# Four experts in two passes, and one of the six weight blocks of a three-pass step multiplied in native fp32 without a split

## The chip, the cores and the metric

The kernel runs on one core of a Trainium2 chip. The metric is the time of one execution on the device, in microseconds, the median of a few runs. One profiled execution gives the trace that is read below.

## What is computed

A two-layer encoder on 256 tokens of width 1024 in fp32: an attention layer and a dense SwiGLU layer, a second attention layer, and a top-2-of-8 mixture of experts. The change lies wholly in the last:

```python
logits = (xt @ w_router).astype(jnp.float32)
top_val, top_idx = lax.top_k(logits, TOP_K)
top_w = jax.nn.softmax(top_val, axis=-1)
...
y = jnp.zeros_like(xt)
for e in range(N_EXPERTS):
    y = y + gates[:, e:e + 1] * swiglu(xt, w_gate[e], w_up[e], w_down[e])
```

Each expert has a gate and an up matrix of 1024 x 3584 and a down matrix of 3584 x 1024. With 8 experts that is 8 x 3 x 3584 x 1024 x 4 bytes = 352.3 MB of weights, each read once.

## The kernel before

**Units.** The weights come in units of 128 x 2048 fp32 (1 MiB). A step is one slice of 512 hidden columns of one expert: two gate units, two up units, two down units. An expert has 7 steps, so the stage has 56 steps and 336 units. SyncE loads the units in the order in which they are used into `raw`, a ring of `RING = 6` buffers. The order is: four gate and up units of step n, then the two down units of step n-1, then the next step. Unit i goes into the buffer of unit i-6.

**Split.** To keep fp32 accuracy on the fast fp32r products, each unit is split in two: ScalarE rounds it to `w_hi` (`hi`, line 623), VectorE subtracts to get `w_lo` (`lo`, line 1169) and counts `lo_done`. The two halves go to one of four places (three in `w_hi`/`w_lo`, a fourth in `qk_hi`/`qk_lo`). ScalarE waits until TensorE has used what stood there (`used`). SyncE waits for `lo_done` of unit i-6 before it loads unit i: the ring buffer is free as soon as it has been split, long before TensorE gets to it.

**Passes.** The tokens of an expert are gathered to at most 96 slots. A three-pass ("big") expert multiplies hi x hi, lo x hi and hi x lo (`three`, lines 1887 to 1889): 12 products of 128x512 for a unit. A two-pass ("small") expert has at most 64 tokens; hi and lo parts of its tokens stand side by side in one 128-wide stationary operand, which takes 8 products for a unit, and a product with a shift matrix (`shifted`, line 2462) that adds the lower half to the upper, twice in a step.

**Order of steps.** A rank by token count picks the experts: five big (`BIG_V`) and three small (`SMALL_V`). `SMALL_AFTER` says behind which big step each small step stands. In iteration n TensorE does gate and up of step n, then down of step n-1 (`step_down`), then the transposes of step n's hidden values (`step_turn`, lines 2341 and 2505). The rows of an expert are gathered and its results added to memory by GpSimd's indirect DMAs (lines 2675 and 2685).

The first step's down units are units 8 and 9, the second's 14 and 15; the second down unit of the step at position n has number 6(n+1)+3.

## Time and profile before

| | |
|---|---|
| median of 3 runs | 1368.86 us (1365.44 to 1369.8) |
| span of the profiled execution | 1365.5 us |
| TensorE busy | 1331.8 us, 98% |
| VectorE busy | 1107.3 us, 81% |
| ScalarE busy | 975.5 us, 71% |
| bytes moved by DMA | 433.24 MB |

The shares are means over the whole span. The expert stage takes the last 63% of it, and it is the stage that counts here: its loads begin at 383.8 us with pauses and run without one from about 490 to 1335 us. TensorE's granted clock is 1.00 in this stage. Matmul records overlap, so the distance from start to start is the cost of one, not its duration.

### The profile page before, as it was taken

What the parts mean: (1) busy time and instruction counts of PE and PEld (TensorE: products, weight loads), DVE (VectorE), ACT (ScalarE), POOL (GpSimd) and SP (SyncE); (2) the same over time, 40 slices, a digit from 0 to 9 for tenths busy, and PEclk for the clock granted to TensorE, in tenths of its full rate; (3) what the DMA queues carried; (4) which work ended last, traced back from release to release, by engine and by line L of the source; (5) the groups of instructions that cost most, each with busy time, mean ns of one, the idle gap of its engine ahead of it and who ended that gap; (6) DMA issues with size and microseconds to landing.
All of it is one profiled execution on the core that took longest, in us unless ns stands there. A gap on an engine that the chain in (4) does not pass through costs nothing.

```text
span 1365.5 us, 18288 instructions
## 1 busy us (share of the span) xinstructions
PE 1331.8 (98%) x7233; PEld 1123.6 (82%) x7233; DVE 1107.3 (81%) x885; ACT 975.5 (71%) x930; POOL 168.7 (12%) x103
## 2 busy tenths in 40 slices
PE   8989999999999999999999999999999999999996
PEld 7888999999999778777877888777877877787784
DVE  4664655555666599999999989999999999999995
ACT  5465544446556667888788878888888888878883
POOL 4251000000000132574400000000000000000001
PEclk8999999999999999999999999999999999999998
DMA  9305755554542389999999999999999999999992
GB/s 372 121 1 185 207 186 184 184 184 154 204 144 86 111 332 401 404 419 407 412 421 419 421 401 390 422 421 421 408 411 421 414 411 421 421 411 422 418 418 98
DMA packets 67203, 433.24 MB, mean 317 GB/s; under 512 B 8160, under 2 KB 10336, under 8 KB 18992
## 3 DMA queue, kind: packets, MB, share of 16 engines
q1 hardware_dynamic: 60320, 418.01, 76.4%
q0 software_dynamic: 3360, 12.22, 3.0%
q10 hardware_dynamic: 3440, 1.91, 0.8%
q8 instruction: 51, 0.84, 0.3%
q14 instruction: 32, 0.26, 0.1%
HBM read 426.09 MB, written 6.03 MB: 316 GB/s over the span
## 4 chain that ended last, share of the span: by engine, by line
PE 74%; DVE 11%; DMA 9%; ACT 4%; issue 1%; SPq 0%; DVEq 0%; ACTq 0%
PE banks L1887 21%; PE banks L1889 20%; PE banks L1888 20%; DMA raw<-in_moe_w_gate 9%; DVE w_lo L1169 6%; ACT w_hi L623 2%; PE banks L2451 2%; DVE qk_lo L1169 2%; PE banks L2120 2%; PE banks L2452 2%; ACT qk_hi L623 1%; PE banks L2108 1%; PE banks L2488 1%; PE banks L2490 1%; PE banks L2462 1%
## 5 line engine op out<-in xcount | busy, mean ns | idle before, releaser
L1169 DVE TENSOR_TENSOR w_lo<-raw,w_hi 128x2048 fp32r<-128x2048 f32 (+1 forms) x312 | 711.2, 2297 | 134.4 <-ACT w_hi L623 132.9
L623 ACT CAST w_hi<-raw 128x2048 fp32r<-128x2048 f32 (+1 forms) x312 | 592.5, 1909 | 161.8 <-PE banks L1889 125.5
L1169 DVE TENSOR_TENSOR qk_lo<-raw,qk_hi 128x2048 fp32r<-128x2048 f32 x84 | 192.0, 2286 | 13.0 <-ACT qk_hi L623 12.1
L623 ACT CAST qk_hi<-raw 128x2048 fp32r<-128x2048 f32 x84 | 160.0, 1905 | 14.3 <-PE banks L1889 9.5
L1887 PE MATMUL banks<-w_hi,t_hi 128*128 128x512 f32 (+2 forms) x444 | 164.7, 371 | 2.9 <-DVE w_lo L1169 1.5
L1889 PE MATMUL banks<-w_lo,t_hi 128*128 128x512 f32 (+2 forms) x444 | 161.6, 364 | 0.0
L1888 PE MATMUL banks<-w_hi,t_lo 128*128 128x512 f32 (+2 forms) x444 | 161.5, 364 | 0.0
L1887 PE MATMUL banks<-t_hi,w_hi 128*128 128x256 f32 x544 | 155.5, 286 | 0.9 <-DVE t_lo L1190 0.9
L1888 PE MATMUL banks<-t_hi,w_lo 128*128 128x256 f32 x544 | 154.3, 284 | 0.0
L1889 PE MATMUL banks<-t_lo,w_hi 128*128 128x256 f32 x544 | 154.2, 284 | 0.0
L1887 PE MATMUL banks<-w_hi,h_hi 128*128 128x512 f32 x300 | 118.8, 396 | 0.2 <-DVE w_lo L1169 0.2
L1889 PE MATMUL banks<-w_lo,h_hi 128*128 128x512 f32 x300 | 117.3, 391 | 0.0
L1888 PE MATMUL banks<-w_hi,h_lo 128*128 128x512 f32 x300 | 117.1, 390 | 0.0
L1887 PEld LDWEIGHTS banks<-t_hi,w_hi 128*128 128x128 f32 x544 | 104.7, 192 | 1.9 <-issue 1.4
L1888 PEld LDWEIGHTS banks<-t_hi,w_lo 128*128 128x128 f32 x544 | 104.7, 192 | 0.4
L1889 PEld LDWEIGHTS banks<-t_lo,w_hi 128*128 128x128 f32 x544 | 104.7, 192 | 0.0
L2451 PE MATMUL banks<-w_hi,t_hi 128*128 128x512 f32 x252 | 101.4, 402 | 2.7 <-DVE w_lo L1169 2.5
L1887 PEld LDWEIGHTS banks<-w_hi,t_hi 128*128 128x128 f32 x444 | 85.8, 193 | 16.2 <-DVE w_lo L1169 1.7
L2452 PE MATMUL banks<-w_lo,t_hi 128*128 128x512 f32 x252 | 98.5, 391 | 0.0
L1889 PEld LDWEIGHTS banks<-w_lo,t_hi 128*128 128x128 f32 x444 | 85.9, 193 | 12.9
L1888 PEld LDWEIGHTS banks<-w_hi,t_lo 128*128 128x128 f32 x444 | 86.0, 194 | 12.1 <-issue 0.2
L2685 POOL DMA_INDIRECT moe_sum<-arena x7 | 12.4, 1772 | 497.8 <-ACT arena L1086 497.8
(358 smaller groups left out, 2261.9 us busy)
## 6 DMA issues: line engine op xcount, KB each, us to landing
raw<-in_moe_w_gate SPq DMA_DIRECT2D x112, 1024.0 KB, 9.9
raw<-in_moe_w_up SPq DMA_DIRECT2D x112, 1024.0 KB, 9.3
raw<-in_moe_w_down SPq DMA_DIRECT2D x112, 1024.0 KB, 9.7
raw<-in_na_w_qkv SPq DMA_DIRECT2D x12, 1024.0 KB, 4.8
raw<-in_ffn_w_gate SPq DMA_DIRECT2D x11, 1024.0 KB, 5.0
raw<-in_ffn_w_up SPq DMA_DIRECT2D x11, 1024.0 KB, 5.1
raw<-in_ffn_w_down SPq DMA_DIRECT2D x11, 1024.0 KB, 4.9
raw<-in_w_in_e SPq DMA_DIRECT2D x6, 1024.0 KB, 15.7
```

Source lines behind the costliest of these rows:

```text
L623: act.copy(tile_hi(u, n), raw[:, u.raw, 0:n]).then_inc(hi_done, 1)
L1169: dve.tensor_tensor(tile_lo(u, n), raw[:, u.raw, 0:n], tile_hi(u, n).bitcast(F32), ALU.subtract).then_inc(lo_done, 1)
L1887: pe.matmul(out, a_hi, b_hi, start=start, stop=False)
L1888: pe.matmul(out, a_lo, b_hi, start=False, stop=False)
L1889: return pe.matmul(out, a_hi, b_lo, start=False, stop=stop)
L2108: last = pe.transpose(banks[:, T_BANK[n % 2], (2 * k + t) * P:(2 * k + t + 1) * P], prob_of(n)[:, b, t * SEQ + k * P:t * SEQ + (k + 1) * P ...
L2120: last = pe.matmul(banks[:, 4 + t, c:c + HD], turned_of(n)[:, (2 * k + t) * P:(2 * k + t + 1) * P], v(k), start=(k == 0), stop=(k == 1))
L2451: pe.matmul(dst, t_small[:, kk, :], hi_w[:, k, :], start=kk == 0, stop=False)
L2452: last = pe.matmul(dst, t_small[:, kk, :], lo_w[:, k, :], start=False, stop=kk == KD - 1)
L2462: pe.matmul(banks[:, 4 + i, :], shift, low[i], start=False, stop=True, skip_group_check=True).then_inc(shift_mm, 1)
L2488: pe.matmul(banks[:, 2 + c, :], lhs, hi_w[:, k, cols], start=j == 0 and i == 0 and k == 0, stop=False)
L2490: last = pe.matmul(banks[:, 2 + c, :], lhs, lo_w[:, k, cols], start=False, stop=j == MOE_STEPS - 1 and i == 1 and k == 1)
```

## The change

There are now four big and four small experts (`BIG_V`, `SMALL_V`, `RANK_OF`), and 28 + 28 steps in place of 35 + 21. The order: four big steps first, then big and small steps in turn, with pairs of small steps between, and three big steps at the end. In the middle no two big steps stand next to each other.

`WHOLE` lists the second down unit of each big step but those of the last two: 26 units. Such a unit isn't split. TensorE multiplies it from its ring buffer in native fp32 with `h_whole`, an fp32 copy of that half of the hidden values; ScalarE and VectorE skip it, and only half of the hidden values is split. Its ring buffer becomes free when TensorE has used it (`used`), so the load six units on waits for that. Counts on `lo_done` and `hi_done` leave these units out, and the four places of split units are dealt among the rest. The low halves of small results (`low_y`) move to another buffer.

```diff
-BIG_V, SMALL_V = (0, 2, 3, 5, 7), (1, 4, 6)
-SMALL_AFTER = ((3, 4, 5, 6, 8, 9, 10), (15, 16, 17, 18, 20, 21, 22), (24, 25, 26, 27, 29, 30, 31))
+BIG_V, SMALL_V = (0, 2, 4, 7), (1, 3, 5, 6)
+SMALL_AFTER = ((3, 4, 5, 6, 7, 8, 8), (9, 10, 11, 12, 13, 13, 14), (15, 15, 16, 16, 17, 17, 18),
+               (19, 20, 20, 21, 22, 23, 24))
...
+WHOLE = [6 * (n + 1) + 3 for n, (v, _) in enumerate(ORDER[:-2]) if v in BIG_V]
+SPLIT = [i for i in range(6 * STEPS) if i not in WHOLE]
...
+    def split(self, ahead=0):
+
+        return self.count(ahead) - self.whole
...
+        h_whole = part_of(8448, 2 * P).rearrange("p (k s) -> p k s", k=2)
...
+            def load_moe(i, src):
+
+                u = moe_unit(i)
+                if i - RING in WHOLE:
+                    sp.wait_ge(used, u.count(-RING))
+                elif i >= RING:
+                    sp.wait_ge(lo_done, moe_unit(i - RING).split())
+                else:
+                    sp.wait_ge(lo_done, u.count(-RING))
+                sp.dma_start(raw[:, u.raw, 0:src.shape[-1]], src).then_inc(raw_full[u.raw], 16)
...
+                elif 6 * (n + 1) + 3 in WHOLE:
+                    act.copy(inner(h_hi, 0)[:, 0:2], turned_in()[:, 0:2])
+                    act.copy(h_whole[:, :, 0:SLOTS], turned_in()[:, 2:4]).then_inc(h_hi_done, 1)
...
+            def step_lo(i):
+
+                if i not in WHOLE:
+                    lo(moe_unit(i))
...
+                elif 6 * (n + 1) + 3 in WHOLE:
+                    dve.tensor_tensor(inner(h_lo, 0)[:, 0:2], turned_in()[:, 0:2], inner(h_hi, 0)[:, 0:2].bitcast(F32),
+                                      ALU.subtract).then_inc(h_lo_done, 1)
...
-                    moe_down(U_MOE, [(0, first_unit + i, 0) for i in range(2)], n, start=j == 0,
-                             stop=j == MOE_STEPS - 1, which=which)
+                    if 0 in which:
+                        moe_down(U_MOE, [(0, first_unit, 0)], n, start=j == 0, which=(0,))
+                    if 1 in which:
+                        u = moe_unit(first_unit + 1)
+                        pe.wait_ge(raw_full[u.raw], u.filled())
+                        for k in range(2):
+                            for c in range(2):
+                                last = pe.matmul(banks[:, c, :], h_whole[:, k, :],
+                                                 raw[:, u.raw, k * D + c * HALF:k * D + (c + 1) * HALF], start=False,
+                                                 stop=j == MOE_STEPS - 1 and k == 1)
+                        last.then_inc(used, 1)
```

SyncE's queue where units 10 to 21 are loaded, before (the second of the two `down` loads is unit 15, and further on unit 21):

```order
L526 DMA raw<-in_moe_w_gate 128x2048 [waits lo_done] x2
L526 DMA raw<-in_moe_w_up 128x2048 [waits lo_done] x2
L526 DMA raw<-in_moe_w_down 128x2048 [waits lo_done] x2
L526 DMA raw<-in_moe_w_gate 128x2048 [waits lo_done] x2
L526 DMA raw<-in_moe_w_up 128x2048 [waits lo_done] x2
L526 DMA raw<-in_moe_w_down 128x2048 [waits lo_done] x2
```

The same place after; line 583 is in `load_moe`:

```order
L583 DMA raw<-in_moe_w_gate 128x2048 [waits lo_done] x2
L583 DMA raw<-in_moe_w_up 128x2048 [waits lo_done] x2
L583 DMA raw<-in_moe_w_down 128x2048 [waits lo_done]
L583 DMA raw<-in_moe_w_down 128x2048 [waits used]
L583 DMA raw<-in_moe_w_gate 128x2048 [waits lo_done] x2
L583 DMA raw<-in_moe_w_up 128x2048 [waits lo_done] x2
L583 DMA raw<-in_moe_w_down 128x2048 [waits lo_done]
L583 DMA raw<-in_moe_w_down 128x2048 [waits used]
```

Units 15 and 21 now wait for `used`, which is TensorE's count, and the loads behind them on the queue wait with them.

TensorE at the end of the first small step's iteration (position 4; `banks` is PSUM, `h_hi` and `h_lo` the hidden values, `tab,arena` the identity and the values to be turned), before: the second down unit of the big step ahead of it, then the small step's transposes (line 2505):

```order
L1889 MATMUL banks<-w_lo,h_hi 128x512
L2462 MATMUL banks<-qk_lo,qk_hi 128x512 [waits low_set]
L1887 MATMUL banks<-qk_hi,h_hi 128x512 [waits lo_done,h_lo_done,h_hi_done]
L1888 MATMUL banks<-qk_hi,h_lo 128x512
L1889 MATMUL banks<-qk_lo,h_hi 128x512
...
L1887 MATMUL banks<-qk_hi,h_hi 128x512
L1888 MATMUL banks<-qk_hi,h_lo 128x512
L1889 MATMUL banks<-qk_lo,h_hi 128x512
L2505 MATMUL banks<-tab,arena 128x64 [waits hid_done]
L2505 MATMUL banks<-tab,arena 128x64 x3
```

The same place after; line 2555 is the native product of `raw` with `h_whole` in `arena`, and line 2565 the transposes:

```order
L1938 MATMUL banks<-qk_hi,h_lo 128x512
L1939 MATMUL banks<-qk_lo,h_hi 128x512
L2512 MATMUL banks<-qk_lo,qk_hi 128x512 [waits low_set]
L2555 MATMUL banks<-raw,arena 128x512 [waits raw_full4]
L2555 MATMUL banks<-raw,arena 128x512 x3
L2565 MATMUL banks<-tab,arena 128x64 [waits hid_done]
L2565 MATMUL banks<-tab,arena 128x64 x3
```

The twelve products of the split unit have become four native ones, behind the same second shift product, and their wait is for the load itself and no longer for VectorE.

## Rows read from the trace of the kernel before

**Rows 1.** The page, part 2: bandwidth moved in 40 slices of 34.1 us.
```profile
GB/s 372 121 1 185 207 186 184 184 184 154 204 144 86 111 332 401 404 419 407 412 421 419 421 401 390 422 421 421 408 411 421 414 411 421 421 411 422 418 418 98
```

**Rows 2.** Windows view: start:end, length, busy us by engine, clock, DMA share, GB/s.
```profile
core 0: us, PE busy (x) PEld busy (x) DVE busy (x) ACT busy (x) POOL busy (x), PEclk, DMA share, GB/s
...
1205.00:1325.00 120.00, 118.81 (x525) 94.23 (x524) 115.45 (x64) 103.04 (x75) 0.00 (x0) 1.00 1.01 421
...
1190.00:1200.00 10.00, 10.00 (x46) 8.19 (x45) 9.21 (x6) 7.96 (x5) 1.97 (x1) 1.00 1.02 381
```

**Rows 3.** DMA issues in 480 to 1366 us: count, median us from issue to landing.
```profile
arena<-x_rows,arena POOLq DMA_INDIRECT x7, 9.4
moe_sum<-arena POOLq DMA_INDIRECT x7, 9.3
```

**Rows 4.** Waits of the SyncE queue, 540 to 1350 us: total, times, longest.
```profile
SPq L526 <- DVE w_lo L1169: 470.8, 230, 3.7
```

**Rows 5.** Groups by form, 540 to 1350 us: busy us, mean ns, idle before.
```profile
L1169 DVE TENSOR_TENSOR w_lo<-raw,w_hi 128x2048 fp32r<-128x2048 f32 x234 | 529.9, 2285 | 25.6 <-ACT w_hi L623 24.0
L623 ACT CAST w_hi<-raw 128x2048 fp32r<-128x2048 f32 x234 | 444.9, 1912 | 71.7 <-PE banks L1889 35.8 <-DMA raw<-in_moe_w_down 15.5 <-DMA raw<-in_moe_w_gate 11.3
```

**Rows 6.** Timeline of one steady cycle: start us, us, engine line op [idle before].
```profile
1253.71 1.91 ACT L623 CAST w_hi<-raw 128x2048 fp32r<-128x2048 f32 x1 [0.57 <-DMA raw<-in_moe_w_down]
...
1258.68 1.92 ACT L623 CAST w_hi<-raw 128x2048 fp32r<-128x2048 f32 x1 [0.52 <-DMA raw<-in_moe_w_gate]
...
1260.62 0.58 ACT L1043 CAST qk_lo<-banks 64x512 fp32r<-64x512 f32 x1
...
1261.26 0.50 PE L2462 MATMUL banks<-qk_lo,qk_hi 128*128 128x512 f32 x1 [0.17 <-ACT qk_lo L1043]
...
1261.60 0.39 PE L1887 MATMUL banks<-qk_hi,h_hi 128*128 128x512 f32 x1
...
1264.14 0.40 PE L1889 MATMUL banks<-qk_lo,h_hi 128*128 128x512 f32 x1
```

**Rows 7.** Timeline of TensorE: the transposes that end the first five later steps.
```profile
508.46 0.33 PE L2341 MATMUL banks<-tab,arena 96*128 96x96 f32 x2
...
525.67 0.33 PE L2341 MATMUL banks<-tab,arena 96*128 96x96 f32 x2
...
543.33 0.41 PE L2341 MATMUL banks<-tab,arena 96*128 96x96 f32 x3
...
557.50 0.40 PE L2505 MATMUL banks<-tab,arena 64*128 64x64 f32 x3
...
572.65 0.33 PE L2341 MATMUL banks<-tab,arena 96*128 96x96 f32 x2
```

**Rows 8.** Line L526 in two windows of one load each: issue time, time to landing.
```profile
L526 SPq DMA_DIRECT2D raw<-in_moe_w_down x1: 327/327/327, 502.3 to 502.3; - x1
...
DMA to landing us min/median/max: 6.7/6.7/6.7
...
L526 SPq DMA_DIRECT2D raw<-in_moe_w_down x1: 338/338/338, 536.0 to 536.0; - x1
...
DMA to landing us min/median/max: 8.6/8.6/8.6
```

**Rows 9.** Tile raw in 380 to 500 us: loads that had the queue nearly alone.
```profile
DMA to landing us min/median/max: 4.7/4.9/7.3
```

**Rows 10.** Line L2052, native fp32 128x512: duration, first and last start, records.
```profile
L2052 PE MATMUL banks<-arena x8: 591/592/593, 57.1 to 60.1; 128*128 128x512 f32 x8
```

**Rows 11.** Timeline of TensorE: end of the last steps and last down product.
```profile
1309.38 0.41 PE L2341 MATMUL banks<-tab,arena 96*128 96x96 f32 x3
...
1326.72 0.25 PE L2341 MATMUL banks<-tab,arena 96*128 96x96 f32 x1
...
1349.46 0.40 PE L1889 MATMUL banks<-qk_lo,h_hi 128*128 128x512 f32 x1
```

More of the change, by code:

```diff
@@ L68, in step_order @@
         for v, after in zip(SMALL_V, SMALL_AFTER):
-            if m in after:
-                order.append((v, after.index(m)))
+            for j, at in enumerate(after):
+                if at == m:
+                    order.append((v, j))
     return order
@@ L90, with whole_before @@
     MOVE_AT.setdefault(max(n for n, w in TURN_AT.items() if w[0] == _v - 1), []).append(_v)
+WHOLE = [6 * (n + 1) + 3 for n, (v, _) in enumerate(ORDER[:-2]) if v in BIG_V]
+SPLIT = [i for i in range(6 * STEPS) if i not in WHOLE]
+def whole_before(i):
+    return sum(1 for w in WHOLE if w < i)
 def turned_count(n):
@@ L183, with __init__ @@
 class Unit:
-    def __init__(self, s, k=0, part=None, behind=PARTS):
-        self.s, self.k, self.own, self.behind = s, k, part, behind
+    def __init__(self, s, k=0, part=None, behind=PARTS, whole=0):
+        self.s, self.k, self.own, self.behind, self.whole = s, k, part, behind, whole
     def count(self, ahead=0):
         return self.k * RING + (self.s + 1 + ahead)
+    def split(self, ahead=0):
+        return self.count(ahead) - self.whole
     def early(self, back):
@@ L334, in trunk @@
         low = [qk_lo[:, 3072 + HALF * i:3072 + HALF * (i + 1)] for i in range(2)]
+        low_y = [t_lo[:, 4 * i:4 * i + 4, P:2 * P] for i in range(2)]
         shift = qk_hi[:, 3584:3584 + P]
@@ L498, in moe_unit @@
         def moe_unit(i):
-            turn = i % (PARTS + 1)
-            return Unit(U_MOE + i, 0, (U_MOE + turn) % PARTS if turn < PARTS else PARTS,
-                        PARTS if i < PARTS else PARTS + 1)
+            q = i - whole_before(i)
+            turn = q % (PARTS + 1)
+            behind = PARTS if q < PARTS else PARTS + 1 if q == PARTS else i - SPLIT[q - PARTS - 1]
+            return Unit(U_MOE + i, 0, (U_MOE + turn) % PARTS if turn < PARTS else PARTS, behind, whole_before(i))
         def unit_of(base, e, c, j=0):
@@ L584, in last @@
                 down(e, MOE_STEPS - 1, base, [(e, 40 + i, 0) for i in range(2)])
-            gate_up(0, 0, U_MOE, [(0, i, 0) for i in range(4)])
+            for i, w in enumerate((moe_w_gate, moe_w_gate, moe_w_up, moe_w_up)):
+                load_moe(i, w[0, 0, i % 2])
             expert = {0: 0}
@@ L601, in _ @@
             with sp.If(n_over > SLOTS):
+                sp.wait_ge(used, U_MOE + E * MOE_UNITS)
                 for again in range(1, SWEEPS):
@@ L1123, in _ @@
                     y_low_copy(n)
[L1124 to L1125 removed]
+                step_hi(6 * n + 3)
+                step_hi(6 * n + 4)
                 if j == 0:
@@ L1166, in lo @@
             def lo(u, n=UNIT):
-                dve.wait_ge(hi_done, u.count())
+                dve.wait_ge(hi_done, u.split())
                 dve.tensor_tensor(tile_lo(u, n), raw[:, u.raw, 0:n], tile_hi(u, n).bitcast(F32),
@@ L1917, in columns @@
             def columns(u, bank, n, transposed, split=None):
-                pe.wait_ge(lo_done, u.count())
+                pe.wait_ge(lo_done, u.split())
                 hi_w, lo_w = unit_parts(u, KD, n)
@@ L1936, in rows @@
             def rows(u, bank, lhs_hi, lhs_lo, n_t, start, stop):
-                pe.wait_ge(lo_done, u.count())
+                pe.wait_ge(lo_done, u.split())
                 hi_w, lo_w = unit_parts(u, 2, D)
@@ L1949, in rows_by_half @@
             def rows_by_half(u, bank, lhs_hi, lhs_lo):
-                pe.wait_ge(lo_done, u.count())
+                pe.wait_ge(lo_done, u.split())
                 hi_w, lo_w = unit_parts(u, 2, D)
@@ L2317, in gate_up @@
                     u = unit_of(base, *units[i])
-                    pe.wait_ge(lo_done, u.count())
+                    pe.wait_ge(lo_done, u.split())
                     hi_w, lo_w = unit_parts(u, 4, HALF)
@@ L2442, in step_gate_up @@
                     u = moe_unit(6 * n - 2 + i if n else i)
-                    pe.wait_ge(lo_done, u.count())
+                    pe.wait_ge(lo_done, u.split())
                     hi_w, lo_w = unit_parts(u, 4, HALF)
@@ L2467, in y_shifts @@
                     pe.wait_ge(y_low_set, 2 * SMALL_V.index(v) + i + 1)
-                    pe.matmul(banks[:, 2 + i, :], shift, low[i], start=False, stop=True, skip_group_check=True).then_inc(y_shift_mm, 1)
+                    pe.matmul(banks[:, 2 + i, :].rearrange("p (k s) -> p k s", k=4), shift, low_y[i], start=False,
+                              stop=True, skip_group_check=True).then_inc(y_shift_mm, 1)
             def step_down(n, which=(0, 1)):
@@ L2481, in step_down @@
                         u = moe_unit(first_unit + i)
-                        pe.wait_ge(lo_done, u.count())
+                        pe.wait_ge(lo_done, u.split())
                         hi_w, lo_w = unit_parts(u, 2, D)
```

74 lines of the change are left out of this document (39 added, 35 removed).

## The prediction

> **What bounds the kernel now.** I read the page's bandwidth row first. From slice 18 on it stands between 390 and 422 GB/s to the end of the stage [rows 1]. The windows view says what that means: over 120 quiet microseconds all 16 DMA engines are busy (share 1.01) at 421 GB/s, and the rate drops, to 381, only in a window that holds one of GpSimd's 14 indirect DMAs [rows 2, 3]. In the steady cycle ScalarE starts on one unit and on the second one after it as they land, at 1253.71 and 1258.68 [rows 6], so a unit takes 2.49 us; 1.0486 MB by 421 GB/s is the same 2.49. The stage's 336 units are 837 us of stream. TensorE (118.8 of 120 us busy) and VectorE (115.5) stand almost as high, but in that window both follow the landings. SyncE's long waits for VectorE [rows 4] are no loss: the loads that it issues queue behind others, and the median indirect DMA too takes 9 us to land. So three engines are nearly full and one of them, DMA, is the floor: what the change takes from TensorE and VectorE buys nothing beyond that floor. What it can do is empty the queue.
>
> **What it takes away.** VectorE loses 26 subtractions of 2.29 us and ScalarE 26 copies of 1.91 us [rows 5], 60 and 50 us. ScalarE copies the hidden values in two pieces instead of one, a few tenths more each. TensorE: twelve products run from 1261.60 to 1264.14 [rows 6], eleven distances, 0.23 us each, 2.8 us for a big unit with the last. A small step has 48 of these in place of 72 and two shift products more, so seven steps more in two passes save 7 x 22 x 0.23 = 35 us. The new operation is there in the trace: line 2052 makes four native fp32 products of 128x512, recorded as eight, with starts from 57.1 to 60.1 [rows 10]: 0.43 us a record, 0.86 a product, 3.43 us for the four of a unit. That is 0.7 us more than the split unit, 26 times: 18 us. TensorE ends up some 17 us shorter. All of this lies beside the stream, and I cost it at nothing. Were the stream no cover, it would be TensorE's 17 us that counted.
>
> The Trainium skill (FP8 and Floating Point Precision, TensorE Precision Notes) gives true fp32 four passes. Four times 0.23 would be 3.7 us for a unit rather than 3.43, and the sum below would be 1.1 us higher; the row shows the product itself, so I stay with it.
>
> **What it adds: a wait of the loads.** Unit 6(n+1)+3 (call it w) now keeps its buffer until TensorE has used it. Load w+6 waits for that, and on SyncE's queue all loads behind it. How late may it be? A load that has the queue nearly alone lands after 4.7 to 4.9 us [rows 9], and w+6 is due 6 x 2.49 = 14.9 us after w. So no DMA time is lost while TensorE ends w within about 10.1 us of w's landing. Two places differ.
>
> *In the middle* a small step follows each big one, and the lag is the least possible. In the cycle of rows 6 w landed at 1256.2 (half way between the two landings shown). Before w TensorE does the second shift product, at 1261.26; it waits for ScalarE's copy at 1260.62, behind the copy of unit w+1, which landed at 1258.68. Splitting w is not on that path. Then w starts at 1261.6, and with 3.43 us it ends at 1265.0, 8.8 us after landing. That leaves 1.3 us of slack. TensorE keeps this lag: behind a big step a small one's iteration took 14.2 us (543.33 to 557.50) and a big one's behind a small one 15.2 (to 572.65) [rows 7]; with 0.7 more the pair takes 30.1 by these rows, against 29.8 for twelve landings. These two iterations hold gather transposes and slot products, about 0.6 us in all; without them it is 29.5. A pair of small steps gives 3 us back. I cost the 22 or so of these waits at nothing. Bounds: nothing, or 1.3 us each if the queue runs less well with two or three loads in it than with four, 29 us. I take nothing, since the load of 502.3 had two others in flight and landed after 6.7 us, and a steady queue is seen with that [rows 8].
>
> *At the start* there are four big steps in a row, and TensorE runs behind. Rows 7 give the ends of units 9, 15, 21 and 27: 508.46, 525.67, 543.33 and 557.50. The load that needs unit 9's buffer was issued after the load of 502.3, at 504.5, and that of unit 27 at 536.0, 7.3 us before TensorE was through with unit 21 [rows 8]. With one native unit more each time these ends become 509.2, 527.1, 545.4 and 560.3. Load 27 can be issued at 545.4 and lands 4.8 later, at 550.2; before, it landed at 536.0 + 8.6 = 544.6. So the stream is 5.6 us behind from there, and lost DMA time never comes back. The earlier two waits are part of this and not added (at the first, unit 14 landed at 509.0, so load 15 comes 2.6 us late). The wait for unit 27 (560.3) is in time: unit 32, before w+6, is now due at 564.7. After that TensorE catches up. Bounds of this term: 2 us, if the delayed loads close up where a gather had slowed them (the two gathers at 520 to 555 cost 2 to 3 us in all), and 7, if each wait adds its own.
>
> The Trainium skill (DMA: Bandwidth & Descriptors, Anatomy of one DMA) puts a DMA's fixed part at about 2.0 us besides its bytes, on GpSimd's path. With 2.0 + 2.49 = 4.5 in place of the 4.8 shown here, the start would cost 0.3 us less.
>
> **The end.** The last three steps are big in both orders. Before, TensorE turned at 1309.38 and 1326.72, 17.3 us apart, and its last product is at 1349.46 [rows 11]: it never waits there. The native unit of the step at position 53 falls in this stretch: 0.7 us. The last two big steps are unchanged. **The adds to memory:** one expert sends 64 rows in place of 96. A window with one such DMA moves 381 instead of 421 [rows 2], 1 us lost; a third less is 0.5 us with the tail of it.
>
> **Sum:** 5.6 + 0.7 - 0.5 = 5.8 us over the profiled execution's 1365.5, so 1371.3 of span. That execution stands 3.4 us below the median of the runs, at their lower end; the same 5.8 on the median of 1368.9 gives 1374.7.
>
> **The rivals.**
> - *A queue that runs thin at every wait* (slower). If a load issued 6 us before its due time doesn't keep 16 engines full, each of 22 waits costs 0.5 to 1.3 us: 11 to 29 us more, 1386 to 1403. It decides once TensorE's lag passes 10.1 us, or the latency of a lone load passes 6.1. Against it: 1.3 us of slack; for it: a stage that has always had four loads in flight, and disturbances (gathers, row transposes) of 0.5 us.
> - *The start costs little* (no change). TensorE's first lag falls in time with the two gathers, which slow the stream anyway; then 2 us or less remain: 1369 to 1371.
> - *The floor gives* (faster). The 421 GB/s may not be DMA's own limit but what is left beside 26 fewer reads of `raw` and writes of both halves; or the indirect DMAs cost less. If the stream became shorter by TensorE's 17 us, it would end at 1374.7 - 17 = 1358. Against it: the rate is 418 to 422 in quiet slices whatever the other engines do [rows 1], and no row shows the stream above 422.
> - *It does something else.* The fourth smallest expert must have at most 64 tokens or all is swept again, at hundreds of microseconds. The reference's router gives 53, 58, 62, 62, 64, 64, 73 and 76 tokens, so it fits.
>
> **How the numbers follow.** Forecast 1374.7, chance 0.50, its own range 1371 to 1378. Start costs little 0.25. Thin queue 0.15. Floor gives 0.09. Something else 0.01. Within 0.3% (about what a measurement of this kernel can tell from no change) is 1364.8 to 1373.0: it takes all of the second case and a quarter of the forecast, 0.37. Faster 0.09, slower 0.38 + 0.15 + 0.01, 0.54. The range leaves out the fast case and the worse half of the thin queue: 1368 to 1390.
>
> **What would show it.** In the trace after: 421 GB/s and DMA share 1 in quiet windows of the middle, and TensorE's idle time risen, VectorE's and ScalarE's too; a dip of the rate between 509 and 550; SyncE waiting for TensorE's line 2555 in the longest waits, with its longest at the start; native records 0.43 us apart; transposes at about 509, 527, 545 and 560; loads issued behind such a wait landing in 5 to 6 us. Wrong would be: dips each 30 us throughout (thin queue), or more than 422 GB/s (the floor gives), or no dip before 550 (start costs little).

## The result, and the profile after

The changed kernel takes 1381.07 us (median of 4 runs, 1378.19 to 1383.48) against 1368.22 us (the median of before with a fourth run): 12.9 us more, ratio 1.0096 with a 95% interval of 1.0077 to 1.0115. The forecast was 1374.7 us, 5.8 more. The direction is right and the time lies inside the wide range of 1368 to 1390, but the loss is more than twice the one forecast.

Its profiled execution has a span of 1381.7 us, 16.2 more than the one of before. That execution is the slowest of its four runs, so the steps below, which are read from the profiles, add up to 16 and not to 13. A span is about 1.8 us shorter than the time of the same execution in all runs here, so by like and like the profiled execution of before stood some 1.6 us under its median, and not the 3.4 of the prediction; the forecast doesn't depend on it.

The page of the changed kernel: span, busy time, bandwidth in 40 slices of 34.5 us, and the chain that ended last.

```profile
span 1381.7 us, 17733 instructions
...
PE 1328.4 (96%) x6977; PEld 1073.1 (78%) x6977; DVE 1046.5 (76%) x858; ACT 938.2 (68%) x945; POOL 125.3 (9%) x103
...
GB/s 372 116 1 183 208 184 188 190 188 155 193 147 62 152 301 356 412 418 398 400 414 411 408 420 410 399 401 407 410 412 415 423 403 405 410 418 418 416 386 131
...
PE 60%; DMA 20%; DVE 10%; ACT 6%; issue 3%; SPq 0%; DVEq 0%; ACTq 0%
DMA raw<-in_moe_w_gate 18%; PE banks L1937 15%; PE banks L1939 15%; PE banks L1938 15%; DVE w_lo L1209 7%; PE banks L2555 6%; ACT w_hi L654 4%; PE banks L2170 2%; DVE qk_lo L1209 2%; PE banks L2501 2%; PE banks L2502 1%; DMA raw<-in_moe_w_up 1%; PE banks L2158 1%; PE banks L2512 1%; ACT qk_lo L1074 1%
```

TensorE, VectorE and ScalarE all have less to do than before, and the program is longer. The bandwidth row says where: in [rows 1] no slice from the 16th on is under 390 until the last; here slice 16 has 356, and of the later ones, which reached 421 again and again, most stay between 398 and 418. The chain of before had DMA at 9%; now it is 20%.

The same in four windows, first of the kernel before, then of the changed one. Columns as in [rows 2]; the last is GB/s, the one before it the busy share of the DMA engines.

```profile
509.00:565.00 56.00, 56.00 (x260) 45.59 (x260) 52.62 (x40) 44.05 (x31) 22.91 (x10) 1.00 1.01 395
565.00:830.00 265.00, 262.79 (x1197) 212.20 (x1196) 251.09 (x167) 220.72 (x161) 67.39 (x21) 1.00 1.01 413
830.00:1090.00 260.00, 257.78 (x1160) 205.74 (x1159) 248.12 (x140) 221.80 (x162) 5.69 (x5) 1.00 1.01 415
1090.00:1300.00 210.00, 207.37 (x921) 163.59 (x920) 201.47 (x114) 179.35 (x128) 2.96 (x2) 1.00 1.01 417
```

```profile
509.00:565.00 56.00, 56.00 (x240) 41.10 (x239) 40.83 (x34) 34.83 (x29) 11.01 (x10) 1.00 0.89 350
565.00:830.00 265.00, 257.08 (x1094) 191.36 (x1093) 230.32 (x157) 208.40 (x164) 31.02 (x20) 1.00 1.01 410
830.00:1090.00 260.00, 249.28 (x1042) 186.09 (x1041) 229.45 (x131) 209.91 (x163) 6.36 (x4) 0.99 1.01 409
1090.00:1300.00 210.00, 204.71 (x862) 151.51 (x861) 183.64 (x107) 168.32 (x133) 4.83 (x3) 1.00 1.01 412
```

At the start of the stage (509 to 565 us) the DMA engines are idle for a tenth of the time, and TensorE is busy in every one of these 56 us: the loads wait for it. Later TensorE is the one with gaps, 5 to 11 us in each window, and yet the stream runs 3 to 6 GB/s slower.

Who holds the loads is in the waits of SyncE's queue (490 to 1350 us: total, times, longest), which answer to [rows 4]:

```profile
SPq L583 <- DVE w_lo L1209: 394.7, 188, 4.4
SPq L583 <- PE banks L2555: 185.8, 26, 10.6
SPq L583 <- DVE qk_lo L1209: 125.3, 61, 3.1
```

26 waits for the native products, 7 us each on average.

For all kernels I use one measure, worked out from issue plus time to landing of the 336 loads: **lateness**, by how much the landings fall behind one unit per 2.487 us. "Start" is from unit 14 to unit 33, "middle" from unit 33 to unit 321. (The trace of before lacks the landing of every sixth unit, 5, 11 and so on to 335; these three are there, and unit 335 is set 2.5 us behind unit 334.) **Lag** is how long after the landing of a held unit w the load w+6 is issued.

| kernel | us | us before, same chip | ratio (95%) | lateness start | middle | median lag, middle |
|---|---|---|---|---|---|---|
| before | | | 1 | 5.4 | 23.3 | not tied |
| after | 1381.07 | 1368.22 | 1.0096 (1.0077 to 1.0115) | 13.0 | 29.7 | 9.0 |
| order only | 1363.95 | 1365.52 | 0.9989 (0.9974 to 1.0005) | 6.8 | 22.0 | not tied |
| native, copied | 1371.51 | 1365.52 | 1.0029 (1.0013 to 1.0045) | 7.2 | 23.7 | not tied |
| split, held | 1371.04 | 1365.52 | 1.0034 (1.0016 to 1.0051) | 12.4 | 23.4 | 8.4 |
| native from unit 27 to 315, held | 1376.55 | 1365.52 | 1.0067 (1.0035 to 1.0100) | 8.7 | 35.4 | 9.2 |
| split, held one unit less | 1367.87 | 1367.59 | 1.0006 (0.9990 to 1.0021) | 8.5 | 22.0 | 5.1 |
| split, held one unit more | 1425.83 | 1367.59 | 1.0441 (1.0410 to 1.0473) | 14.1 | 71.8 | 11.7 |
| native 9, 15, 21, 27, held | 1370.80 | 1367.59 | 1.0038 (1.0021 to 1.0054) | 12.1 | 22.2 | not tied |
| native in the old order, held | 1398.31 | 1367.59 | 1.0221 (1.0179 to 1.0262) | 12.8 | 42.9 | 9.4 |
| native, own buffer | 1371.54 | 1367.36 | 1.0037 (1.0023 to 1.0052) | 13.0 | 21.0 | not tied |
| split, own buffer | 1364.71 | 1367.36 | 0.9984 (0.9971 to 0.9997) | 7.7 | 21.2 | not tied |
| native from 27 to 315, own buffer | 1364.28 | 1367.27 | 0.9991 (0.9977 to 1.0005) | 4.8 | 21.7 | not tied |

A ratio leaves out executions far above the rest: one of 2621.5 us among the twelve of "native, own buffer", for which no trace was kept, and one of 1457.8 us, at a lower clock, among those of before.

Lateness is read from one profiled execution of each kernel. Its time lies 6.6 us above the kernel's median in "native from unit 27 to 315, held", 4.5 above in "order only", 3.2 below in "native, copied", and within 3.4 us in the others. So differences of one or two us between two kernels are read with care, and prices of parts are taken from the ratios as well.

The profiles of before and after then split up so: landings of unit 14 +0.5, start 13.0 - 5.4 = 7.6, middle 29.7 - 23.3 = 6.4, units 321 to 335 +3.8, and what follows the last landing -2.3 (26.2 us against 28.5). The sum is 16.0 of the 16.2.

The three ideas that the experiments had to tell apart: (A) the order; (B) the native product, 0.7 us longer on TensorE; (C) the held buffer, which puts the next load behind TensorE.

### The profile page after: what moved, and what is told of

It is laid out like the page before. It is cut to its first block, busy times and chain, and to the rows that moved or that the text cites. A ratio compares the mean times of both kernels' runs of the same rounds, so it can differ in the third digit from the quotient of the medians.

```text
span 1381.7 us, 17733 instructions
## 1 busy us (share of the span) xinstructions
PE 1328.4 (96%) x6977; PEld 1073.1 (78%) x6977; DVE 1046.5 (76%) x858; ACT 938.2 (68%) x945; POOL 125.3 (9%) x103
## 4 chain that ended last, share of the span: by engine, by line
PE 60%; DMA 20%; DVE 10%; ACT 6%; issue 3%; SPq 0%; DVEq 0%; ACTq 0%
DMA raw<-in_moe_w_gate 18%; PE banks L1937 15%; PE banks L1939 15%; PE banks L1938 15%; DVE w_lo L1209 7%; PE banks L2555 6%; ACT w_hi L654 4%; PE banks L2170 2%; DVE qk_lo L1209 2%; PE banks L2501 2%; PE banks L2502 1%; DMA raw<-in_moe_w_up 1%; PE banks L2158 1%; PE banks L2512 1%; ACT qk_lo L1074 1%
## 5 line engine op out<-in xcount | busy, mean ns | idle before, releaser
L1209 DVE TENSOR_TENSOR w_lo<-raw,w_hi 128x2048 fp32r<-128x2048 f32 (+1 forms) x293 | 671.1, 2300 | 197.3 <-ACT w_hi L654 195.7
L654 ACT CAST w_hi<-raw 128x2048 fp32r<-128x2048 f32 (+1 forms) x293 | 557.2, 1907 | 201.5 <-PE banks L1939 102.4
L654 ACT CAST qk_hi<-raw 128x2048 fp32r<-128x2048 f32 x77 | 146.7, 1905 | 39.2 <-DMA raw<-in_moe_w_gate 14.9
L2501 PE MATMUL banks<-w_hi,t_hi 128*128 128x512 f32 x336 | 135.6, 404 | 5.4 <-DVE w_lo L1209 4.3
L1937 PE MATMUL banks<-w_hi,t_hi 128*128 128x512 f32 (+2 forms) x360 | 130.4, 362 | 5.3 <-DVE w_lo L1209 2.9
L1939 PE MATMUL banks<-w_lo,t_hi 128*128 128x512 f32 (+2 forms) x360 | 128.4, 357 | 0.0
L1938 PE MATMUL banks<-w_hi,t_lo 128*128 128x512 f32 (+2 forms) x360 | 128.3, 356 | 0.0
L2555 PE MATMUL banks<-raw,arena 128*128 128x512 f32 x208 | 93.5, 592 | 0.0
L2501 PEld LDWEIGHTS banks<-w_hi,t_hi 128*128 128x128 f32 x336 | 63.1, 188 | 27.2 <-DVE w_lo L1209 13.8
L1937 PEld LDWEIGHTS banks<-w_hi,t_hi 128*128 128x128 f32 x360 | 69.9, 194 | 15.2 <-DVE w_lo L1209 3.1
L1939 PEld LDWEIGHTS banks<-w_lo,t_hi 128*128 128x128 f32 x360 | 69.9, 194 | 9.4
L2502 PEld LDWEIGHTS banks<-w_lo,t_hi 128*128 128x128 f32 x336 | 63.2, 188 | 12.1
L1937 PE MATMUL banks<-w_hi,h_hi 128*128 128x512 f32 x180 | 71.4, 397 | 0.6 <-DVE w_lo L1209 0.3
## 6 DMA issues: line engine op xcount, KB each, us to landing
raw<-in_moe_w_down SPq DMA_DIRECT2D x112, 1024.0 KB, 10.6
```

Source lines behind the costliest of these rows:

```text
L654: act.copy(tile_hi(u, n), raw[:, u.raw, 0:n]).then_inc(hi_done, 1)
L1209: dve.tensor_tensor(tile_lo(u, n), raw[:, u.raw, 0:n], tile_hi(u, n).bitcast(F32), ALU.subtract).then_inc(lo_done, 1)
L1937: pe.matmul(out, a_hi, b_hi, start=start, stop=False)
L1938: pe.matmul(out, a_lo, b_hi, start=False, stop=False)
L1939: return pe.matmul(out, a_hi, b_lo, start=False, stop=stop)
L2501: pe.matmul(dst, t_small[:, kk, :], hi_w[:, k, :], start=kk == 0, stop=False)
```

## Experiments: which of the three parts costs

**The order alone.** All units split and released as before; the new order, the fourth small expert and its 64-row add stay.

```
-WHOLE = [6 * (n + 1) + 3 for n, (v, _) in enumerate(ORDER[:-2]) if v in BIG_V]
+WHOLE = []
```

> The changed kernel with every unit split in two again (no native product, no held buffer): the order of steps and the four two-pass experts alone. Theory 'held buffers' (the loss of 13 us comes from loads that wait until TensorE has used a whole unit): the stream runs as before, 1366 to 1370, ratio to before 0.998 to 1.002. Rival 'order' (four two-pass experts or the new order bring the indirect DMAs into worse places): most of the loss stays, 1376 to 1381.

Measured: 1363.95, ratio 0.9989 (0.9974 to 1.0005). So (A) costs nothing that can be measured, and its seven steps fewer in three passes gain nothing that stands outside the interval either. This is the base for the rest.

**Native product without the held ring buffer.** ScalarE copies the unit whole into free columns, and the ring buffer is released after the copy.

```
+                if i in COPIED:
+                    act.wait_ge(raw_full[u.raw], u.filled())
...
+                    act.copy(part_of(1536, 1536), raw[:, u.raw, 0:1536])
+                    act.copy(part_of(4096, 512), raw[:, u.raw, 1536:UNIT]).then_inc(hi_done, 1)
```

> The changed kernel, but ScalarE copies the whole unit in fp32 to a free stretch of the arena, VectorE only counts it, and the ring buffer is free after the copy, as with split units; TensorE's native product is the same, read from the copy. Theory 'held buffers': 1367 to 1371. Rival 'native price' (the native product costs TensorE more than its cover, whoever holds the buffer): 1377 to 1382.

Measured: 1371.51, ratio 1.0029, just above the 1367 to 1371 of the theory. The landings show little of it: start 7.2 and middle 23.7, as in the order alone within 2 us, and 31.1 us behind the last landing in place of 29.1. These two profiled executions are equally long (spans of 1366.5 and 1366.6 us) though the medians are 7.6 us apart, so they can't show the whole of it.

**Held buffer without the native product.** All units split, but the 26 loads wait for TensorE.

```
                 if i - RING in WHOLE:
                     sp.wait_ge(used, u.count(-RING))
+                elif i - RING in HELD:
+                    sp.wait_ge(used, u.count(-RING) + 0)
```

> The changed kernel's order with every unit split and multiplied in three passes, but the load six units after the second down unit of each three-pass step (the same 26 loads) waits until TensorE has used that unit, though it doesn't need to. Theory 'held buffers': most of the loss comes back without any native product: 1375 to 1381, a little less than the change, since TensorE is 0.7 us earlier each time. Rival 'native price': 1367 to 1370.

Measured: 1371.04, ratio 1.0034, between the two expectations; the theory had asked for about twice the loss. The start's lateness rises from 6.8 to 12.4, the 5.6 us of the prediction, and the middle loses next to nothing (23.4 against 22.0). Two windows and the wait:

```profile
509.00:565.00 56.00, 56.00 (x259) 45.36 (x258) 49.51 (x39) 41.37 (x29) 17.60 (x10) 1.00 0.98 382
565.00:830.00 265.00, 254.20 (x1135) 198.37 (x1134) 252.97 (x166) 226.22 (x165) 35.40 (x20) 1.00 1.01 413
```

```profile
SPq L588 <- PE banks L1942: 168.7, 26, 9.9
```

The same 26 waits, nearly as long, leave 413 GB/s here and 410 in the changed kernel. What differs is 0.6 us of lag, 8.4 against 9.0, about what the native product adds. So the held buffer alone pays the price of the start, and next to nothing in the middle.

**Held and native, from unit 27 to unit 315.** Of the 26, the 22 whose step is followed by a small one; units 9, 15, 21 and 327 are split.

```
+WHOLE = [i for i in SECOND if ORDER[i // 6][0] in SMALL_V]
```

> The change with 22 whole units in place of 26: units 9, 15 and 21, behind which TensorE still works through the run of big steps at the start, and unit 327 in the run at the end are split. Theory 'start and end, then a thin queue': the start gives back 6 to 8 us and the end 0.7, 1372 to 1375, while the middle keeps its 6. Rival 'only the start matters': 1367 to 1370. Rival 'every wait costs alike' (22/26 of 13 stay): 1379.

Measured: 1376.55, ratio 1.0067, above what I expected. In the profile the middle alone is 13.4 us later than with the order alone (35.4 against 22.0), but that is the slowest of five executions, and by the ratios the loss is 0.8%, 10.6 us. The changed kernel, with the same 22 waits, has 29.7: of the 5.7 us between the two, 4.0 have come about by unit 69. Here the stream isn't held up by units 9 to 21, so TensorE, behind from the four big steps, is further behind it when the first held loads are due (lags of 13.9, 10.7 and 10.1 us at loads 33, 45 and 57, where the changed kernel has 9.7, 9.0 and 9.8). Even so, the waits that the prediction cost at nothing carry a large part.

**Held and native in units 9, 15, 21 and 27 only.**

```
+WHOLE = [9, 15, 21, 27]
```

> Native, unsplit product and held buffer in the first four three-pass steps alone (units 9, 15, 21 and 27), all others split; new order. Theory of separate parts: the start costs 5 to 8 us and the middle its own part (the run with the 22 others alone came to 9 over the kernel before): 1370 to 1374 us, ratio 1.003 to 1.006. Rival (the start decides nearly all of it and leaves a thin queue that the middle then cannot fill): 1375 to 1381, ratio 1.007 to 1.011.

Measured: 1370.80, ratio 1.0038. Start 12.1, middle 22.2: what is lost at the start leaves nothing behind it. Against the order alone the ratios say +0.5% for the start, +0.8% for the middle, and the whole change is +1.1%; each difference of two ratios is known to 0.2 to 0.4 only, and within that they add up.

## Experiments: how late a load may be issued

**Held one unit less.** All split; the load waits until TensorE has used the unit ahead of w, and until w is split.

```
+                elif i - RING in HELD:
+                    sp.wait_ge(lo_done, moe_unit(i - RING).split())
+                    sp.wait_ge(used, u.count(-RING) + -1)
```

> All products split, the new order, nothing native; the 26 loads that go into the place of a second down unit w of a three-pass step wait until the unit ahead of w is multiplied (and w is split), one unit earlier than in the run that held the buffer until w itself was used. That run lost 5 us, all of it in the first steps, at a mean lag of 8.2 us from the landing of w to the load's release; here the lag should be about 5.5. Theory (a load must be issued about 9.0 us after w's landing at the latest, and only what passes that is lost): the restart after the routing costs about half of what it did, nothing is lost later: 1365 to 1369 us, ratio 1.000 to 1.003. Rival (the loads lose by being tied to TensorE at all, through bunching): again 1370 to 1372, ratio 1.003 to 1.005.

Measured: 1367.87, ratio 1.0006. The queue waits for TensorE 26 times, 3.3 us each, and nothing is lost in the middle (22.0). Being tied to TensorE isn't what costs.

```profile
SPq L584 <- PE banks L1943: 86.2, 26, 7.1
```

**Held one unit more.**

```
+                    sp.wait_ge(used, u.count(-RING) + 1)
```

> The same with the buffer held one unit longer than needed: the load waits until TensorE has used the unit behind w as well. The lag becomes about 8.2 + 2.5 = 10.7 to 11.1 us, which is over the 9.0 that the changed kernel's trace seems to allow, in every one of the 26 places. Theory: in the middle most steps now lose up to 2 us each until TensorE has so much less work waiting that the lag falls to about 9; 1385 to 1410 us, ratio 1.014 to 1.03. If the limit were the 10.1 us of the prediction, the middle would lose under 1 us a step: 1376 to 1390. If only the start were sensitive to the holding time: 1373 to 1377.

Measured: 1425.83, ratio 1.0441, beyond the upper end of my own theory. The middle's lateness is 71.8. The lag came out at 11.7 and not at 10.7 to 11.1, above the 9.0 as well as the 10.1 us between which the run was to decide, so it doesn't tell them apart. The windows show idle DMA engines, which the changed kernel shows only at the start:

```profile
565.00:830.00 265.00, 244.80 (x1067) 189.26 (x1066) 237.14 (x157) 211.54 (x155) 39.52 (x20) 0.98 0.96 387
830.00:1090.00 260.00, 236.23 (x1010) 179.97 (x1009) 231.00 (x130) 210.58 (x157) 5.72 (x4) 0.97 0.97 391
```

One of its waits, by line L588 in two windows of one load each (issue, time to landing):

```profile
L588 SPq DMA_DIRECT2D raw<-in_moe_w_down x1: 333/333/333, 790.1 to 790.1; - x1
...
DMA to landing us min/median/max: 10.6/10.6/10.6
...
L588 SPq DMA_DIRECT2D raw<-in_moe_w_down x1: 333/333/333, 812.5 to 812.5; - x1
...
DMA to landing us min/median/max: 4.8/4.8/4.8
```

Unit 117 lands at 790.1 + 10.6 = 800.7, load 123 is issued 11.7 us later and lands 4.8 after that, 16.5 after unit 117, where 14.9 was due.

All held loads between units 39 and 315 of the six kernels whose middle loads wait for TensorE (133 loads), by lag, with what the load before was late taken off the lag:

| lag, us | loads | issue to landing, mean | late, mean | late by over 0.4 |
|---|---|---|---|---|
| under 7 | 21 | 9.8 | 0.0 | 0% |
| 7 to 8.75 | 31 | 6.6 | 0.1 | 10% |
| 8.75 to 9.25 | 43 | 5.9 | 0.1 | 7% |
| 9.25 to 9.75 | 9 | 5.9 | 0.5 | 44% |
| 9.75 to 10.25 | 6 | 6.1 | 1.1 | 50% |
| 10.25 to 11.25 | 11 | 5.3 | 1.1 | 91% |
| over 11.25 | 12 | 5.6 | 2.6 | 100% |

A load that lands when it is due has taken 14.9 us less its lag, whatever the queue does: at a lag of 9.0, 5.9 us. So the third column is no cause of its own while loads are in time. What the table shows is where lateness begins: under 9.25 us hardly a load is late, from there to 10.25 half of them, above it nearly all. There is no one limit. In the old order (next run) load 291 was issued 9.8 us after unit 285 landed, with two other loads in flight:

```profile
L585 SPq DMA_DIRECT2D raw<-in_moe_w_down x1: 333/333/333, 1247.9 to 1247.9; - x1
...
DMA to landing us min/median/max: 5.1/5.1/5.1
```

9.8 + 5.1 = 14.9, and it was in time. Load 159 of the changed kernel had the same lag and the same two ahead, took 6.1 us and was 1.1 us late. Of the loads between 9.25 and 10.25, those in time took 5.1 to 5.6 us, the late ones 6.0 to 7.6.

GpSimd's indirect DMAs explain a part of this. With none in flight beside the load, 3 of 72 loads with a lag under 9.25 are late by over 0.4 us, 4 of 10 up to 10.3, and 12 of 13 above; these last land 4.7 to 5.2 us after their issue, as a lone load does, which puts the point from which they are late at 9.7 to 10.2. With one in flight it is 3 of 24, 4 of 5 and 9 of 9, at up to 7.8 us to landing. What slowed the others, such as load 57 of the changed kernel (6.2 us), isn't shown.

**The old order with native, held units.** Seven more held buffers, and big steps that follow each other.

```
-BIG_V, SMALL_V = (0, 2, 4, 7), (1, 3, 5, 6)
+BIG_V, SMALL_V = (0, 2, 3, 5, 7), (1, 4, 6)
```

> The order of the kernel before (five experts in three passes, three in two), with the native, unsplit second down unit in every three-pass step but the last two: 33 or so held buffers instead of 26, and three-pass steps that follow each other. Theory (every held buffer costs about the same, since the order by itself cost nothing): 13 us times 33/26 and some more where two held steps follow each other: 1381 to 1389 us, ratio 1.012 to 1.017. Rival (alternating steps are what lets TensorE catch up, so that held buffers in a row are worse than held buffers apart): 1390 to 1405, ratio 1.018 to 1.029.

Measured: 1398.31, ratio 1.0221, which is the rival. In the trace the two largest losses stand behind big steps in a row: unit 123 lands 4.9 us late at a lag of 12.8, unit 237 5.6 us late at 12.9. Both also had indirect DMAs beside them and took 7.0 and 7.7 us to land with no load ahead. So the order of the change, which gains nothing by itself, is worth 17 us with native, held units: 1.0221 against 1.0096. Its seven held buffers fewer are part of that; by the count alone, at 13 us for 26, they would be 3.5 (an estimate).

## Experiments: the held buffer taken away

**All 26 native, loaded into a seventh buffer.** 2048 columns of the arena are free by then. The unit's place in the ring stays empty, so the load behind it needs no wait for TensorE, while the product is the one of the changed kernel.

```
+                if i in WHOLE:
+                    k = WHOLE.index(i)
+                    if k:
+                        sp.wait_ge(used, moe_unit(WHOLE[k - 1]).count())
...
+                    sp.dma_start(whole_buf, src).then_inc(whole_full, 16)
+                    return
```

> The changed kernel with the same 26 native products, but each of these 26 units is loaded into a seventh buffer of its own (2048 columns of the arena that are free by then), which waits only until the one before it is used; their places in the ring stay empty, so no load waits for TensorE and SyncE gets one unit further ahead. Theory (the held ring buffer is what empties the queue, the native product by itself costs TensorE 0.7 us each, of which some 4 us show): 1364 to 1371 us, ratio 0.997 to 1.003, and the sum of late landings between units 33 and 321 back from 29.7 to 22 to 24 us. Rival (the native product itself, by putting TensorE later, makes the landings late): still over 1375, ratio over 1.005.

Measured: 1371.54, ratio 1.0037, just above what was expected (up to 1.003). The middle is back at 21.0, but the start is not, at 13.0. SyncE's waits and the windows say why:

```profile
SPq L588 <- PE banks L2570: 27.0, 3, 10.6
```

```profile
509.00:565.00 56.00, 56.00 (x238) 41.52 (x238) 40.50 (x28) 34.66 (x27) 10.99 (x10) 1.00 0.95 372
565.00:830.00 265.00, 258.55 (x1105) 193.98 (x1104) 234.16 (x158) 211.70 (x165) 30.05 (x20) 1.00 1.01 416
```

In the first four steps the native units are six loads apart, so the one extra buffer is asked for again just when the ring buffer was: three waits, 9 us each, as long as those they replace. From then on they are twelve or eighteen apart and nothing waits.

**Native from unit 27 to 315 in the seventh buffer.** The 22 products of the run at 1.0067.

```
+WHOLE = [i for i in SECOND if ORDER[i // 6][0] in SMALL_V]
...
+                            pe.wait_ge(whole_full, 16 * (WHOLE.index(first_unit + 1) + 1))
+                            whole = whole_buf
```

> Native second down unit in the 22 steps of the middle only (33 to 315, alternate steps), each loaded into the seventh buffer, so that no load waits for TensorE anywhere; the first four and the last three-pass step split. The same 22 products with the ring buffer held came to 1.0067 of the kernel before. In the run with all 26 in the seventh buffer the only waits left for TensorE were three in the start, 27 us in all, and the lateness there was that of the changed kernel (13.0 against 5.4), while the middle was back at 21 us. Theory (the whole loss is the waits of the loads for TensorE; a native product by itself costs next to nothing where it lies in the middle): 1364 to 1368 us, ratio 0.998 to 1.0015, lateness 6 to 8 at the start and 21 to 23 in the middle. Rival (the native products cost some 4 us by themselves, as the run with the copied units at 1.0029 seems to say): 1369 to 1372, ratio 1.002 to 1.004.

(The 22 begin at unit 27; the text on record says 33.) Measured: 1364.28, ratio 0.9991 (0.9977 to 1.0005), where the theory had put it. The middle's lateness is 21.7, against 35.4 with the same products from a held ring buffer. The bandwidth:

```profile
509.00:565.00 56.00, 56.00 (x252) 44.27 (x251) 49.07 (x32) 41.61 (x30) 16.80 (x10) 1.00 1.01 400
565.00:830.00 265.00, 261.55 (x1126) 197.77 (x1125) 235.57 (x159) 211.76 (x167) 37.20 (x20) 1.00 1.01 414
830.00:1090.00 260.00, 249.38 (x1044) 183.74 (x1042) 230.63 (x133) 212.34 (x168) 5.12 (x4) 1.00 1.01 416
```

So (B) costs nothing in the middle as long as no buffer is held for it. (C) alone cost 1.4 us there (23.4 against 22.0), and the two together 7.7 (29.7 against 22.0): the loss needs the held buffer, and in it the 0.6 us that the native product adds to the lag.

**All split, second down units in the seventh buffer.** The deeper queue without native products. The 26 loads are those of the run with all 26 native, with one wait changed, and the split reads from the new buffer.

```
-                        sp.wait_ge(used, moe_unit(WHOLE[k - 1]).count())
+                        sp.wait_ge(lo_done, moe_unit(SEVENTH[k - 1]).split())
...
-                act.copy(tile_hi(u, n), raw[:, u.raw, 0:n]).then_inc(hi_done, 1)
+                act.copy(tile_hi(u, n), (raw[:, u.raw, 0:n] if u.own_raw is None else whole_buf)).then_inc(hi_done, 1)
```

> Everything split into two fp32r parts, in the new order (the run of the order alone came to 0.9989 of the kernel before), but the 26 second down units are loaded into the seventh buffer, so the queue is one unit deeper behind each of them for half the cycle. Theory (lead is worth something: a deeper queue takes up some of the disturbances that the kernel before pays for, 23 us in the middle and 5 to 7 at the start): 1360 to 1365 us, ratio 0.996 to 0.9995. Rival (those disturbances are lost transfer time on the DMA engines and no depth of the queue brings them back): 1364 to 1367, ratio 0.9985 to 1.001.

Measured: 1364.71, ratio 0.9984 (0.9971 to 0.9997). This is the only kernel here whose interval lies below 1, by 2.2 us on the ratio, less than the 0.3% that the prediction called measurable. Its middle (21.2) and start (7.7) don't differ from those of the order alone, so I don't claim that depth brought it: the extra buffer does not win back the disturbances of before.

## Why the prediction was right and wrong

1. **The floor: right.** The stream sets the end in every kernel that doesn't hold it up: TensorE gained 3 to 9 us of gaps in each long window and nothing came of them, and the order alone, with fewer products, came to 0.9989.

2. **The start, 5.6 us: mechanism right, size near.** By the two profiles it is 7.6 us, over ten of them 6.3. Timeline of TensorE in the changed kernel, the last native record and the transposes behind it:

```profile
510.02 0.59 PE L2555 MATMUL banks<-raw,arena 128*128 128x512 f32 x1
510.45 0.33 PE L2391 MATMUL banks<-tab,arena 96*128 96x96 f32 x2
...
528.30 0.33 PE L2391 MATMUL banks<-tab,arena 96*128 96x96 f32 x2
...
546.70 0.33 PE L2391 MATMUL banks<-tab,arena 96*128 96x96 f32 x2
```

Forecast were 509.2, 527.1 and 545.4. The two distances are 17.85 and 18.4 us where [rows 7], with 0.7 added, gave 17.9 and 18.3; the whole row is 1.2 to 1.3 us late because the stage began so in this execution (the first of its transposes stands at 498.4 against 497.1 before). It stands at 497.1 to 499.0 in the six profiles in which TensorE's granted clock was at its lower level, 1.2 GHz, for 10.2 us from about 19 us on, long before the experts, and at 493.0 to 494.8 in the seven others; so it goes with whole executions and is no effect of the change. Line L583, loads 15, 27 and 33:

```profile
L583 SPq DMA_DIRECT2D raw<-in_moe_w_down x1: 327/327/327, 510.6 to 510.6; - x1
...
DMA to landing us min/median/max: 5.1/5.1/5.1
...
L583 SPq DMA_DIRECT2D raw<-in_moe_w_down x1: 339/339/339, 546.9 to 546.9; - x1
...
DMA to landing us min/median/max: 5.0/5.0/5.0
...
L583 SPq DMA_DIRECT2D raw<-in_moe_w_down x1: 343/343/343, 561.6 to 561.6; - x1
...
DMA to landing us min/median/max: 8.2/8.2/8.2
```

Load 27 landed at 551.9, 7.3 us later than before, where 550.2 and 5.6 were forecast; 1.3 of the difference is the stage's own start. The fourth wait lost nothing, as forecast: unit 32 came 2.5 us before load 33's 569.8. Over the five kernels whose loads wait until units 9 to 21 are used (13.0, 12.4, 12.8, 12.1, 13.0) and the five without a wait there or at unit 27 (5.4, 6.8, 7.2, 7.7, 4.8) the start's lateness differs by 6.3 us on average. The estimate of 4.5 us for a lone megabyte, made with the fixed part of about 2.0 us that the Trainium skill (DMA: Bandwidth & Descriptors, Anatomy of one DMA) gives for GpSimd's path, is a little low for these loads of SyncE: they took 5.0 and 5.1, and 4.7 to 5.2 in the undisturbed ones of the longest-held run.

3. **The middle, 0 us: this step failed.** It is 6.4 us by the profiles. The wait, its place and the steady lag were forecast well (8.8 us, and it is 9.0). What failed is "That leaves 1.3 us of slack" and the zero that was put on 22 waits for it. The 1.3 us set one steady lag against the landing time of a load that nothing disturbs, 4.8 us [rows 9]. For such a load the 10.1 us holds (late from 9.7 to 10.2 us on, above). But the lag went up to 9.85 us, and the three held loads that were late in the middle took 6.1 to 7.7 us, so at just these places no slack was left. Rows 8 warned of it: 6.7 us with two loads in flight, which I quoted as a reassurance without the subtraction. 14.9 - 6.7 = 8.2 is under the lag of 8.8; it is no limit either, as that load was landing when it was due, but 4.8 was not the figure to rest on. The native product's 0.7 us, cost at nothing because it lies beside the stream, is part of the same failure: with the lag 0.6 us shorter, in the run split and held, the same waits cost 1.4 us and not 7.7. One such place, units 51 and 57:

```profile
L583 SPq DMA_DIRECT2D raw<-in_moe_w_down x1: 339/339/339, 604.2 to 604.2; - x1
...
DMA to landing us min/median/max: 10.4/10.4/10.4
...
L583 SPq DMA_DIRECT2D raw<-in_moe_w_down x1: 342/342/342, 624.4 to 624.4; - x1
...
DMA to landing us min/median/max: 6.2/6.2/6.2
```

Landed at 614.6, released 9.8 us later, landed 6.2 after that at 630.6, where 629.5 was due: inside the 10.1 of the prediction, and 1.1 us late all told (0.8 of it this load's own; the load before was 0.3 late). Of the 21 held loads from unit 39 to 315, three are more than 0.5 us late (57, 159 and 189: 0.8, 1.1 and 0.7), 18 are in time; all together 2.9 us. The remaining 3.5 of the 6.4 fall on loads that wait for nothing on TensorE. They are the held buffer's doing too, since the middle is back at 21.0 and 21.7 without it, but how they come about (a thin queue that no longer covers a disturbance, or the bunched issue behind a wait) no run here tells apart.

TensorE's clock doesn't explain the 6.4 us. It fell to its lower level, half of full speed, twice in this stretch, for 3.4 us each from 902.5 and 984.4, which the kernel before doesn't show. Both times TensorE had just stood idle, 2.9 and 2.1 us:

```profile
902.34 0.71 PE L2512 MATMUL banks<-qk_lo,qk_hi 128*128 128x512 f32 x1 [2.93 <-ACT qk_lo L1074]
...
902.50:905.90 3.40, 3.40 (x9) 2.56 (x9) 3.24 (x3) 2.84 (x3) 1.94 (x1) 0.50 1.03 436
```

The fall comes behind the late loads, and the next held loads, 177 and 207, were in time. In the run held one unit more the clock fell six times in the middle, 27 us in all; what that adds to the loss there is not told apart.

4. **The end, 0.7 us: small, as said.** Measured is 1.5: units 321 to 335 land 3.8 later (load 333 by 4.5, held until TensorE, 12.5 us behind, was through with unit 327), of which 2.3 come back since TensorE was behind there anyway. That this hold would delay a landing at all was not in the working.

5. **The native product: its length right, its price only where no buffer is held for it.** Its records:

```profile
L2555 PE MATMUL banks<-raw,arena x208: 590/592/595, 507.0 to 1342.5; 128*128 128x512 f32 x104
```

592 ns as in [rows 10], and by the timeline eight records start 0.43 us apart, 3.4 us a unit. Costing it at nothing in the middle is borne out by the run at 0.9991, but not with the ring buffer held (point 3). With 26 of them and ScalarE's copies the ratio was 1.0029; what these some 5 us against the order alone are isn't settled (2.0 stand behind the last landing and 1.7 in the middle, by the two profiles that don't show the whole).

6. **The 64-row add, -0.5 us:** not seen apart; it is within the interval of the order alone.

The rival that came true in part is the thin queue. It named two signs: a lag over 10.1 us, which the changed kernel's middle doesn't reach, and a landing time over 6.1 us for a lone load, which its three late loads pass, though with two others ahead of them. It was wrong in its price for each wait: 18 of 21 cost nothing, and three cost about 1 us. Its 0.15 was too little against a slack of 1.3 us that rested on one row.

## What to carry to other kernels

Before a ring buffer is held longer, take ring x time per unit, subtract the lag, and compare what is left with the time to landing of a load beside the worst disturbance of the stream, not with that of a load alone. Of the 14.9 us here, holding was free in the middle at lags of 5.1 us and all but free at 8.4, began to cost at disturbed places at 9.0, and cost at nearly every wait at 11.7. An operand that must stay longer than the others belongs in a buffer outside the ring, and only where the buffer isn't asked for again one ring later. Work taken off engines that follow a stream bought nothing here, and in the middle work added to TensorE cost nothing, as long as no load waited for it.

## What the runs showed of the hardware

- The busy share of the DMA engines, at two decimals, does not show a loss of one or two per cent: it is 1.01 at 409 GB/s in the changed kernel's middle as at 415 before. With longer gaps it falls: 0.89 at the start (350 GB/s) and 0.96 in the run held one unit more (387).
- A megabyte load with one load ahead of it landed 4.7 to 5.2 us after its issue where nothing disturbed it. Among the 133 held loads it took 5.1 to 7.7 with two ahead (6.0 in the middle of them) and 9.7 with three. While a load is in time this is only the time left until it is due; it became a limit where an indirect DMA of GpSimd or another disturbance ran beside it.
- The loss by lag is steep: 3.3 us more of it (8.4 to 11.7) made a kernel that lost 1.4 us in its middle lose 50.
- TensorE's granted clock fell to half for 3.4 us at a time inside the expert stage, right behind 2 to 3 us in which TensorE had nothing to do (902.5 and 984.4 us in the changed kernel).
